# Prompt attention of a two-layer decoder step: the units of a head pair in another order

## The reference

```python
s = jnp.einsum('btngd,btknd->btkng', qg, kg).reshape(bx, t, k, h).astype(jnp.float32) + bias
s = jnp.where(valid[..., None], s, -jnp.inf)
lse = jax.nn.logsumexp(s, axis=2)
p = jnp.exp(s - lse[:, :, None, :])
o = jnp.einsum('btkng,btknd->btngd', p.astype(vg.dtype), vg)
```

## Time and profile before

| what | value |
|---|---|
| median of 3 runs | 1676.34 us (1674.63 to 1677.95) |
| the profiled execution | 1670.8 us, span 1669.0 us |
| PE busy | 1547.9 us (93%) |
| DVE, ACT, POOL busy | 695.3, 658.3, 737.2 us |
| mean granted TensorE clock | 0.96 |

### The profile page before, as it was taken

How to read it: one execution, slowest core, us unless ns; L and a number is a source line. 1 busy time by engine, 2 the same in 40 slices (tenths; PEclk the granted TensorE clock), 3 DMA queues, 4 the chain that set the end, 5 groups by cost and what they waited for, 6 DMA issues and landing times.

```text
span 1669.0 us, 31025 instructions
## 1 busy us (share of the span) xinstructions
PE 1547.9 (93%) x12182; PEld 1480.2 (89%) x12182; DVE 695.3 (42%) x1180; ACT 658.3 (39%) x1083; POOL 737.2 (44%) x414
## 2 busy tenths in 40 slices
PE   7999978699999999999989986877999999999998
PEld 6999876499999999999979774766999999999998
DVE  4154354226343434212442863667454443432224
ACT  4233554214434344222554553545234434432234
POOL 3645550014444444444435555664434444444444
PEclk9999979779999999999989996999999999999999
DMA  4222331212223322333223221111223223223333
GB/s 166 91 90 67 116 122 64 90 43 88 88 88 89 95 92 88 102 97 102 82 85 116 87 66 59 34 52 38 76 78 99 88 88 100 89 88 101 101 100 116
DMA packets 52836, 146.89 MB, mean 88 GB/s; under 512 B 5485, under 2 KB 18057, under 8 KB 52250
## 3 DMA queue, kind: packets, MB, share of 16 engines
q1 hardware_dynamic: 51386, 139.27, 26.4%
q10 hardware_dynamic: 1376, 6.62, 1.1%
HBM read 139.11 MB, written 6.76 MB: 87 GB/s over the span
## 4 chain that ended last, share of the span: by engine, by line
PE 79%; DVE 9%; ACT 3%; DMA 3%; POOL 2%; issue 2%; SPq 2%; ACTq 0%; DVEq 0%; POOLq 0%
PE PS L644 66%; DVE act_lo L1569 2%; DMA w_raw<-in_w 2%; PE PS L730 2%; PE PS L1010 2%; PE PS L709 1%; PE PS L988 1%; DVE pC L1596 1%; PE PS L718 1%; PE PS L660 1%; DVE xC L1588 1%; POOL q_loC L610 1%; PE PS L1043 1%; SPq L366 1%; POOL sq L624 1%
## 5 line engine op out<-in xcount | busy, mean ns | idle before, releaser
L483 POOL TENSOR_TENSOR w_lo<-w_raw,w_hi 128x1024 fp32r<-128x1024 f32 x217 | 534.1, 2461 | 845.1 <-ACT w_hi L1172 845.1
L644 PE MATMUL PS<-act_hi,w_hi 128*128 128x260 f32 x2592 | 744.1, 287 | 25.4 <-DVE act_lo L1569 12.4
L644 PE MATMUL PS<-act_lo,w_hi 128*128 128x260 f32 x2592 | 736.3, 284 | 0.0
L644 PE MATMUL PS<-act_hi,w_lo 128*128 128x260 f32 x2592 | 735.4, 284 | 0.0
L644 PEld LDWEIGHTS PS<-act_hi,w_hi 128*128 128x128 f32 x2592 | 492.0, 190 | 40.3 <-issue 27.5
L1172 ACT ACTIVATE w_hi<-w_raw 128x1024 fp32r<-128x1024 f32 x217 | 230.0, 1060 | 730.2 <-PE PS L644 709.7
L644 PEld LDWEIGHTS PS<-act_lo,w_hi 128*128 128x128 f32 x2592 | 492.7, 190 | 0.4
L644 PEld LDWEIGHTS PS<-act_hi,w_lo 128*128 128x128 f32 x2592 | 492.7, 190 | 0.0
L644 PE MATMUL PS<-h_hi,w_lo 128*128 128x260 f32 x704 | 198.8, 282 | 0.0
L644 PE MATMUL PS<-h_hi,w_hi 128*128 128x260 f32 x704 | 198.6, 282 | 0.0
L644 PE MATMUL PS<-h_lo,w_hi 128*128 128x260 f32 x704 | 198.5, 282 | 0.0
(11 more groups left out here) (310 smaller groups left out, 1831.3 us busy)
## 6 DMA issues: line engine op xcount, KB each, us to landing
w_raw<-in_w SPq DMA_DIRECT2D x217, 512.0 KB, 3.5
kcA<-in_cache_k SPq DMA_DIRECT2D x8, 512.0 KB, 4.9
biasC<-scratch_rows SPq DMA_DIRECT2D x16, 256.0 KB
vcA<-in_cache_v SPq DMA_DIRECT2D x6, 512.0 KB, 5.2
x<-in_xT SPq DMA_DIRECT2D x4, 520.0 KB, 5.9
out_y<-x SPq DMA_DIRECT2D x8, 260.0 KB, 3.8
biasA<-scratch_rows SPq DMA_DIRECT2D x8, 256.0 KB
kcC<-in_pool_k SPq DMA_DIRECT2D x16, 128.0 KB, 2.5
```

Of the source, the lines that this page charges most:

```text
L483: pool.tensor_tensor(w_lo[:, s, :], w_raw[:, s, :], w_hi[:, s, :].bitcast(F32), ALU.subtract).then_inc(S("w_lo"), 1)
L644: mm = pe.matmul(PS[:, 2 * place + half, 0:HALF], w[:, s, j * P:(j + 1) * P], r[:, c, cols], start=first and n == 0 and i == 0, stop=last ...
```

## The change

The order of a pair's eight units is written out in a table. It alternates the two heads, and a wide query block with a narrow one; the widths in blocks are 4, 1, 3, 2, 2, 3, 1, 4 where they were 1, 2, 3, 4, 1, 2, 3, 4. The waits that counted units of the old order are moved: a head's bias buffer and value tile become free after its last unit (unit 6 of the pair for head 0, unit 7 for head 1), and both heads' biases are waited for at the pair's first two units (`FIRST`). The first output product of a pair alone now carries the flag that clears the bank (`start`), since the first unit has four of them.

```diff
-            return [(p, par, qb) for p in range(pairs) for par in range(2) for qb in range(QB)]
+            return [(p, par, qb) for p in range(pairs) for par, qb in TURNS]
+
+        TURNS = ((0, 3), (1, 0), (0, 2), (1, 1), (0, 1), (1, 2), (0, 0), (1, 3))
+        FIRST = TURNS[0:2]
...
-                            sp.wait_ge(S("t_x"), BASE_A + 8 * (p - 2) + 4 * par + 6)
+                            sp.wait_ge(S("t_x"), BASE_A + 8 * (p - 2) + par + 9)
...
-                            sp.wait_ge(S("C_bm"), 8 * (p - 2) + 4 * par + 4)
+                            sp.wait_ge(S("C_bm"), 8 * (p - 2) + par + 7)
...
-                        pool.wait_ge(S("t_v"), 8 * (pair - 2) + 4 * par + 6)
+                        pool.wait_ge(S("t_v"), 8 * (pair - 2) + par + 9)
...
-                if qb == 0:
+                if (par, qb) in FIRST:
                     pool.wait_ge(S(f"bias{p % 2}{par}"), 16 * (p // 2) + 48)
...
-                    if par == 0 and qb == 0:
+                    if (par, qb) == TURNS[0]:
                         staged(p)
...
-                    if par == 0 and qb == 0:
+                    if (par, qb) == TURNS[0]:
                         pe.wait_ge(S("t_o"), base // 8 + p + 1)
...
-                                       pt[:, i % 2, kb * P:(kb + 1) * P], start=i % 8 == 0,
+                                       pt[:, i % 2, kb * P:(kb + 1) * P], start=i % 8 == 0 and kb == 0,
...
-                if qb == 0:
+                if (par, qb) in FIRST:
                     dve.wait_ge(S(f"bias{p % 2}{par}"), p // 2 * 16 + 16)
```

## The result

The changed kernel takes 1687.61 us (median of 4 runs, 1685.38 to 1689.70), the kernel before in the same job 1676.65. The ratio is 1.0066, 95% interval 1.0049 to 1.0084: 11.0 us slower, between 8 and 14. The forecast was 3.9 us slower, with an upper end of 1683.5. The direction came out, the size did not.

What follows compares the result with a forecast made beforehand. In layer C's attention no engine is full; a chain through several sets the pace. A 0 and C +.7 -.5 -1.0 -.25 +5.0, taken as +3.9 on 1676.34, gave 1680.2 us, range 1677.5 to 1682.5.

Steps and rivals of the forecast that it cites:

- A: 0: Layer A's attention: three later pairs -.1 us, start +.2, together taken as 0.
- C, pair 4's bias: +5.0: Layer C, pair 4: the second head's bias, wanted sooner, lands behind the first head's, adding a second wait, +5.0 us.
- the free transfer: Pair 4 of C: second bias load runs beside the first, leaving at most +.5 us; the forecast's sum then -.6.
- The double wait also lowers PE's clock: Rival, pair 4 of C: a second stalled stretch at low clock costs 1.4 us more, 1681.6 us; chance .17.
- C, the start: +.7: Layer C's first scores, four blocks instead of one, covered by nothing: between 0 and +1 us, taken as +.7.
- six pairs -.5: Layer C's six pairs with query staging on POOL: about -.1 us a pair, together -.5.
- the sample work -1.0: Layer C, sample group's work at fixed steps: between -1.3 and +.6 us, taken as -1.0.
- the last pair -.25: Layer C's last pair, without query staging: from add 7 to add 2, 4.98 us instead of 5.22, so -.25.
- may hide: Layer C: the sample group's PE work at step 5 meets a stretch bound by DVE and POOL; taken as -1.0 us.
- The sample work's base: Layer C, pairs 1 and 2 before: 17.07 us a pair against 16.43, so sample work costs .64 each.
- At nothing: Later release of head 0's bias, A's value copies, start flag and moved waits: no cost, no further bias waits.
- The alternation pays: Rival, twelve pairs: buffers get 10 and 10 blocks instead of 12 and 8, .7 us a pair, -8.4; chance .12.

Runs made afterwards that it cites:

- a_only: Changed kernel with the new order in layer A only, layer C and its waits as before: 1675.98 us, ratio 1.0007 to the kernel before.
- after_warm: Changed kernel with filler transposes on idle TensorE before and at C's start and behind units 32 to 34: 1679.75 us, ratio 1.0039 to the kernel before.
- narrow: Changed kernel with heads alternating the other way round, widths 1 4 2 3 3 2 4 1: 1671.40 us, ratio 0.9980 to the kernel before.
- after_rows4: Changed kernel with the table of bias rows written four times instead of twice: 1667.41 us, ratio 0.9954 to the kernel before.
- before_rows4: Kernel before, old order, with the table of bias rows written four times instead of twice: 1663.14 us, ratio 0.9940 to the kernel before.
- after_early: Changed kernel with pair 4's two bias loads issued ahead of the value pages of samples 6 and 7: 1677.00 us, ratio 1.0017 to the kernel before.
- before_early: Kernel before with pair 4's two bias loads issued ahead of the value pages of samples 6 and 7: 1672.70 us, ratio 0.9983 to the kernel before.
- old_first: Changed kernel with pair 0 of both layers in the old order: 1683.79 us, ratio 1.0047 to the kernel before.
- swap_end: Changed kernel with a pair's last two units exchanged, widths 4 1 3 2 2 3 4 1: 1675.13 us, ratio 1.0005 to the kernel before.
- narrow_end: Changed kernel with widths 1 4 2 3 3 2 1 4, a wide unit last: 1686.97 us, ratio 1.0069 to the kernel before.
- before_rows8: Kernel before, old order, with eight copies of the table of bias rows: 1661.63 us, ratio 0.9926 to the kernel before.

## Why the prediction was right or wrong

- **A: 0.** Right in the sum. a_only costs 1.2 us with an interval that holds 0. The three later pairs came out at +.1 for -.1, but by +.2, +.2 and -.3, so partly by luck; the start at about +.5 for +.2. 12.44 us for the last pair is within the .3 of 12.7 that the forecast named.
- **C, pair 4's bias: +5.0.** Right for its own step: from the add of unit 7 to that of unit 2 the pair takes 1119.95 - 1104.89 = 15.06 us, before 1106.46 - 1096.25 = 10.21, a difference of 4.85. The rate behind one another held (5.39 us for 5.9), and the free transfer, the lower bound, did not come.
- **The double wait also lowers PE's clock.** This rival, at +1.4 and a chance of .17, came true beside the forecast: after_warm takes 1.5 us out of pair 4 by keeping PE busy. I argued that place_q covers much of it; it did not.
- **C, the start: +.7.** Mis-sized: +2.6, or 14.73 to 14.82 in four traces of the new order against 12.23 to 12.59 in six of the old. Only the longer first scores were priced. 1.1 us are the low clock, 1.5 remain at full clock. What makes up the 1.5 stays open: unit 0 is alone in the pipe, and its add, exponential, scale, T and O are four blocks each, but narrow, whose unit 0 has one block and whose unit 1 has four, starts in 14.43 to 14.60 us.
- **C, six pairs -.5, the sample work -1.0, the last pair -.25.** Here lies the larger half of the miss: these pairs sum to 103.40 us against 99.59 before, +3.8 instead of -1.75. Two steps failed. The first is a term put at nothing: the sum prices every pair at one clock, and the rival has a low clock only behind pair 4. At a granted clock of 1.00 pairs 1 to 3 and 5 to 7 take 16.66, 16.54, 16.82, 16.75, 18.03 and 14.85 us in the new order (after_warm, in pairs 2 and 3 after_rows4) and 16.72, 16.65, 16.41, 16.43, 17.30 and 15.31 in the old (before_rows4 in pairs 1 and 2, before): +.8. So some 3.0 of the 3.8 us are low clock; this split is read from other executions of the same pairs, not from an edit. The second is "may hide": the sample work does not hide. At full clock the new order costs +.4, +.3 and +.7 in pairs 3, 5 and 6, and -.1, -.1 and -.5 in pairs 1, 2 and 7. In pair 3 a product stands in front of unit 4's scores, as shown above; in pair 5 one stands in front of unit 0's, which come 2.76 us after the add of unit 7 and before 1.65; in pair 6 eight small operations on VectorE follow a scale that lasts 1.54 us beside the four-block bm of the next pair, before .64 beside one of one block. In pair 4 the products (i = 36 and 39) stand in front of other units, and with its bias in time the forecast's -.1 came out: 16.33 us in after_early, 16.41 in before_early, both at full clock.
- **The sample work's base** was misread too: the .64 us each in pairs 1 and 2 held stretches at low clock. At full clock these pairs cost .3 more than pair 3 in the old order (before_rows4) and nothing more in the new (old_first: 16.79 and 16.59 against 16.80). And pair 5, the plain pair of the forecast, carries sample products itself (i = 42 and 45), as pair 3 does (24 and 27).
- **At nothing.** Right: no wait for a bias in pairs 5 to 7 or in A.
- **The alternation pays.** As a statement on this change it is out. Its price, .7 us a pair, is what narrow gains in pair 3. Its reason, the blocks of the two buffers, is not the cause: swap_end gives its two buffers 13 and 7 blocks, narrow_end 7 and 13, and the one has the shortest pair (15.33) and the other the longest (17.02).

The terms as measured, .5 for A, 2.6 for the start, 6.5 for pair 4, 3.8 for the other pairs and .4 behind the last, sum to 13.8 in the profiled executions; the medians give 11.0, up to 14. The difference is within the scatter of the starts and of the low-clock stretches from run to run, and is left open at that.

## What to carry to other kernels

When the order of units in a software pipeline changes, price each unit by what stands behind it on its engine: a wide unit is cheap where others fill the wait, and dear in the last place, where its own step ends the group. At the start of layer C all four alternating orders were dearer than the ascending one. Side work that stands at fixed steps meets other units in the new order, so price it there again. Price every step at the clock that the stretch has, and count what a longer wait does to that clock after it. And before an order is changed because of a late load, look at how the load is spread: here one dimension of its source was worth as much as the best order, 12.4 us in before_rows8 (.9926).

## What the runs showed of the hardware that was not expected

The table of bias rows was changed for pair 4, but 13 us of its gain lie ahead of the attentions. In the changed kernel, as in the one before, the chain ahead of A goes through SP, which spends microseconds on single issues while the loads of the biases (L369) are under way, and then through a late weight load; ahead of C it goes through one that takes 16 us, where the page gives 3.5 as the median (start us, us, what):

```profile
162.21 5.51 SPq L369
...
167.76 5.00 SPq L400
...
173.70 10.28 DMA w_raw<-in_w
...
983.29 15.97 DMA w_raw<-in_w
```

In after_rows4 the chain holds none of these rows: the first scores of A come at 218.39 instead of 225.00 (216.3 to 218.6 in the five runs with four or eight copies, 222.2 to 225.0 in all others), and from A's last add to C's first scores 753.0 us pass instead of 759.1 (751.1 to 753.0, and 758.1 to 761.4). So a load on few DMA engines costs time far from the place that waits for it. How is not shown: the weights may wait for their part on the same engines, or behind SP's long issues; no run separates the two, and none shows the single engines.

A filler that does nothing but keep TensorE busy gained 4.5 us. And a PE that the profile shows busy is not yet at full clock: it was busy for 9.19 of the first 10 us of A in the changed kernel and stayed at 1.2 GHz all through them.
